# Mixture-of-experts start: an earlier place for the first expert's down weights, and its input gathered transposed in two halves

## What is computed

```python
h = h + hybrid_mixer(rms_norm(h, norm1_g[layer]), w_in[layer], ret_norm_g[layer], hgrn_norm_g[layer], w_out[layer], lb)
h = h + expert_choice_ffn(rms_norm(h, norm2_g[layer]), w_router[layer], w_gate[layer], w_up[layer], w_down[layer])

def expert_choice_ffn(xn, w_router, w_gate, w_up, w_down):
    affinity = jax.nn.softmax((xn @ w_router).astype(jnp.float32), axis=-1)
    gate, idx = lax.top_k(jnp.swapaxes(affinity, 1, 2), cap)          # 16 experts, 32 tokens each
    xe = jax.vmap(lambda xb, ib: xb[ib])(xn, idx)                     # the chosen rows
    hid = silu(einsum('becd,edf->becf', xe, w_gate)) * einsum('becd,edf->becf', xe, w_up)
    ye = einsum('becf,efd->becd', hid, w_down) * gate[..., None]
    return scatter_add(ye, idx)
```

## Time and profile before

| | us |
|---|---|
| median of 3 runs (1631.9 to 1633.9) | 1632.93 |
| profiled execution, its own time | 1631.66 |
| span of that execution in the trace | 1629.5 |
| PE busy | 1307.9 |
| PE weight loads busy | 924.8 |
| DVE busy | 575.2 |
| ACT busy | 455.2 |
| POOL busy | 137.7 |

### The profile page before, as it was taken

The page is one execution under the profiler, slowest core; times in us unless marked ns, Lnnn a source line. Parts: engine busy times, 40 slices in busy tenths (PEclk is TensorE's granted clock), DMA queues, the critical chain, the costliest instruction groups (busy, mean ns, idle before and its releaser), DMA issues.

```text
span 1629.5 us, 28377 instructions
## 1 busy us (share of the span) xinstructions
PE 1307.9 (80%) x12516; PEld 924.8 (57%) x12516; DVE 575.2 (35%) x879; ACT 455.2 (28%) x592; POOL 137.7 (8%) x169
## 2 busy tenths in 40 slices
PE   8999999999999987566566667999987566566565
PEld 7788889998989843223222233989853223222232
DVE  7984774765484520000000002584520001000001
ACT  6337653445555311001010012554311001010011
POOL 0220200000313000000000000304000000000000
PEclk9999999999999999989899788999999989898887
DMA  8334344545445899999999999335899999999997
GB/s 280 105 129 156 117 173 157 205 160 203 156 147 216 369 422 427 427 429 429 428 428 429 429 428 403 134 123 226 351 420 426 428 428 428 430 427 430 427 427 302
DMA packets 79504, 515.59 MB, mean 316 GB/s; under 512 B 6545, under 2 KB 6929, under 8 KB 54593
## 3 DMA queue, kind: packets, MB, share of 16 engines
q1 hardware_dynamic: 76000, 509.21, 76.7%
q0 software_dynamic: 912, 2.83, 0.5%
q10 hardware_dynamic: 2512, 2.36, 0.4%
HBM read 513.33 MB, written 1.05 MB: 316 GB/s over the span
## 4 chain that ended last, share of the span: by engine, by line
DMA 47%; PE 37%; DVE 10%; ACT 2%; issue 2%; SPq 1%; DVEq 0%; ACTq 0%
DMA board<-in_w_down 24%; DMA board<-in_w_gate 21%; PE dense L1769 7%; PE dense L1771 7%; PE dense L1770 7%; PE bank L2340 4%; PE bank L2370 2%; DVE ring_parts L1288 2%; ACT ring_parts L887 2%; DMA ring<-in_even_w_in 1%; DVE board L1572 1%; DVE board L1563 1%; PE dense L1792 1%; PE bank L2163 1%; PE bank L2310 1%
## 5 line engine op out<-in xcount | busy, mean ns | idle before, releaser
L2340 PE MATMUL bank<-ring,board 128*32 128x256 f32 x2688 | 209.6, 463 | 142.7 <-DMA ring<-in_w_up 87.0
L2340 PEld LDWEIGHTS bank<-ring,board 128*32 128x32 f32 x2688 | 91.0, 125 | 255.4 <-DMA ring<-in_w_up 108.1
L1111 ACT ACTIVATE board<-bank 128x256 f32<-128x256 f32 x32 | 12.3, 384 | 731.7 <-PE bank L2340 731.7
L1682 DVE TENSOR_TENSOR board<-board,bank 128x256 f32<-128x256 f32 x32 | 13.5, 421 | 554.3 <-ACT board L1111 554.3
L1288 DVE TENSOR_TENSOR ring_parts<-ring,ring_parts 128x4096 fp32r<-128x4096 f32 (+1 forms) x41 | 172.6, 4213 | 84.8 <-ACT ring_parts L887 84.7
L887 ACT ACTIVATE ring_parts<-ring 128x4096 fp32r<-128x4096 f32 (+1 forms) x47 | 161.5, 3438 | 117.0 <-DMA ring<-in_w_in 30.1
L1769 PE MATMUL dense<-board_parts,ring_parts 128*128 128x256 f32 x624 | 179.4, 287 | 0.6 <-DVE ring_parts L1288 0.6
L1771 PE MATMUL dense<-board_parts,ring_parts 128*128 128x256 f32 x624 | 176.6, 283 | 0.0
L2340 PE MATMUL bank<-board 128*32 128x256 f32 x1408 | 108.0, 459 | 69.6 <-DMA board<-in_w_up 40.9
L1769 PEld LDWEIGHTS dense<-board_parts,ring_parts 128*128 128x128 f32 x624 | 119.7, 192 | 2.1 <-issue 1.9
L2340 PEld LDWEIGHTS bank<-board 128*32 128x32 f32 x1408 | 51.1, 124 | 122.7 <-DMA board<-in_w_up 50.5
(11 more groups left out here) (354 smaller groups left out, 2067.7 us busy)
## 6 DMA issues: line engine op xcount, KB each, us to landing
ring<-in_w_gate SPq DMA_DIRECT2D x44, 2048.0 KB, 40.8
ring<-in_w_up SPq DMA_DIRECT2D x40, 2048.0 KB, 41.8
ring<-in_w_down SPq DMA_DIRECT2D x40, 2048.0 KB, 40.8
board<-in_w_up SPq DMA_DIRECT2D x24, 2048.0 KB, 40.7
board<-in_w_gate SPq DMA_DIRECT2D x20, 2048.0 KB, 41.2
board<-in_w_down SPq DMA_DIRECT2D x20, 2048.0 KB, 40.7
ring<-in_w_in SPq DMA_DIRECT2D x18, 2048.0 KB, 7.9
ring<-in_even_w_in SPq DMA_DIRECT2D x9, 2048.0 KB, 7.9
```

What stands on the lines that cost most here:

```text
L2340: last = mm(o.rearrange("p (m b) -> p m b", b=2), xeT[:, 4 * (j // 2) + k, :], cols.rearrange("p (m r b) -> p r m b", r=2, b=2)[:, q % 2], ...
```

## The change

Three things. (1) `rgT` moves from columns 4096 to 5120 of the work area to the first half of the columns of `xT` (from 17920), and `m_hi` becomes a list of four quarters, at 2048, 2560, 3072 and 15872; so neither lies in the place of unit 4 any more. (2) Unit 4's load waits for the last input projection alone. (3) The first expert's rows are gathered already turned: x is the weight operand (128 x 128, every eighth feature) and `cselr` the moving one (32 columns), eight products for each half of the features, straight into the layout of `xeT`; DVE multiplies each half by the gain. The second half is gathered between the first expert's units 0 and 1. The copy, the two transposes and the old gather of the first expert fall away.

```diff
-        rgT = area(4096, "p (h s) -> p h s", h=RH, s=S)
+        rgT = board[:, WORK:WORK + RH * S].rearrange("p (h s) -> p h s", h=RH)
-        m_hi = work_r[:, 2048:4096].rearrange("p (c s) -> p c s", c=8)
+        m_hi = [work_r[:, at:at + 512].rearrange("p (c s) -> p c s", c=2) for at in (2048, 2560, 3072, 15872)]
...
-                        if s == RING:
-                            sp.wait_ge(gm_sb, 4 * (l + 1))
-                        sp.wait_ge(*((unit_done, OUT2[l] + 1), (rp_ps, RH * (l + 1)), (ho_ps, l + 1), (lg_ps, l + 1))[s - RING])
+                        sp.wait_ge(*((unit_done, OUT2[l]), (rp_ps, RH * (l + 1)), (ho_ps, l + 1), (lg_ps, l + 1))[s - RING])
...
+                        high = m_hi[2 * k + b]
...
-                        own.link(v.tensor_copy(m_hi[:, both, :], mT[:, both, :]))
-                        tt(m_lo[:, both, :], mT[:, both, :], m_hi[:, both, :].bitcast(F32), ALU.subtract).then_inc(gm_sb, 1)
+                        own.link(v.tensor_copy(high, mT[:, both, :]))
+                        tt(m_lo[:, both, :], mT[:, both, :], high.bitcast(F32), ALU.subtract).then_inc(gm_sb, 1)
...
+                def first_input(half):
+
+                    dve.wait_ge(*((xe_ps, NE * l + 1) if half else (ge_ps, (NE + 1) * l + 2)))
+                    k = slice(4 * half, 4 * half + 4)
+                    tt(xeT[:, k, :], WB[1][:, 128 * half:128 * half + 128].rearrange("p (k c) -> p k c", k=4), g2[:, k, :],
+                       ALU.mult).then_inc((ge_sb, xe_sb)[half], 1)
...
-                chosen_rows(0)
-                expert_input(0)
+                first_input(0)
+                first_input(1)
                 choose(1)
...
+                def gather_turned(half):
+
+                    for k in range(4 * half, 4 * half + 4):
+                        for i in range(NT):
+                            last = mm(WB[1][:, CAP * k:CAP * k + CAP], x[:, i, :].rearrange("p (m k) -> p k m", k=DC)[:, k],
+                                      cselr[:, i, :], start=i == 0, stop=i == 1)
+                    last.then_inc((ge_ps, xe_ps)[half], 1)
...
-                    pe.wait_ge(xe_sb, one)
+                    pe.wait_ge(*((ge_sb, NE * l + 1) if first else (xe_sb, one)))
                     for j in range(4):
                         w = in_place(j)
+                        if first and j == 1:
+                            gather_turned(1)
+                        if first and j == 2:
+                            pe.wait_ge(xe_sb, one)
...
-                gather(0)
-                gathered(0)
+                pe.wait_ge(csel_sb, NE * l + 1)
+                gather_turned(0)
                 for e in range(HEAD_E):
-                    expert(e, 6 * e)
+                    expert(e, 6 * e, first=e == 0)
```

More of the change, by code:

```diff
@@ L2274, in _ @@
                     chunks = range(4 - 4 * n, 8 - 4 * n)
-                    rows_unit(OUT2[l] + n, [[t[:, c, :] for c in chunks] for t in (m_hi, m_lo)], n == 0, n == 1,
+                    rows_unit(OUT2[l] + n, [[m_hi[c // 2][:, c % 2, :] for c in chunks], [m_lo[:, c, :] for c in chunks]], n == 0, n == 1,
                               [[], [], [bank_read, at(mix_transposes, 0)], []] if n == 0 else [[], [], [], [first_rows]],
@@ L2320, in gathered, with expert @@
                     last.then_inc(xe_ps, 1)
-                def expert(e, j0, turn=None, more=True):
+                def gather_turned(half):
[4 more added lines that the diff above has]
+                    last.then_inc((ge_ps, xe_ps)[half], 1)
+                def expert(e, j0, turn=None, more=True, first=False):
                     one = e + (NE * l + 1)
```

## The result

The changed kernel takes 1639.38 us (median of 6 runs, 1637.7 to 1639.85) against 1632.6 of the kernel before: ratio 1.0038, interval [1.0028, 1.0048], so 0.38% slower; the medians lie 6.8 us apart. The forecast was 1632.2, with a range up to 1634.3.

The account below looks back on a forecast made before the run. The prediction took the expert stretches to be bound by the weight stream at about 428 GB/s. A gain of 0.36 us in each layer, 0.7 in all, off the 1632.93 median gave 1632.2 us, range 1630.0 to 1634.3.

Parts of the forecast that it names:

- The slower rival: Turned gather: weights 32 bytes apart double the loads; first products 1.6 us later, 5.0 us lost, 1637.9 us; chance 0.1.
- The prediction's own sign of being wrong: First expert's gather: a first half over 3.46 us and a dip behind unit 12 would show a slower outcome.
- the price of a half of the gather: Eight products on PE: 3.1 us for the first half, bounds 1.96 and 3.56; 1.96 for the second at full clock.
- one place of x per nanosecond: Old gather's strided reading: 128 pairs in 128 ns, against 122 ns per router load, so stride may cost nothing more.
- the clock: PE in the first expert's gather: granted clock 0.50 until 577.5 us, then 1.00.
- a cover that went: Second half of the gather: unit 12 issued 3.79 us after 11, hidden by the 4.9 us unit 11 feeds the stream.
- 0.36 us gained at 11: First expert's input: first products start 3.48 us after 574.31, 0.36 us earlier per layer; bounds 1.51 earlier, 0.10 later.
- The part that I priced at nothing: Unit 4's load, some 11 us earlier: closes the first dip, but gains nothing if the first products end as late.
- the two gates: Weight stream held by unit 4's load and by the end of the first expert's unit 0 on PE, which issues 11.

Follow-up runs that it names:

- run with eight times the columns: Changed kernel with the turned gather's moving operand repeated eight times, 256 columns instead of 32, same result; 1638.41 us, ratio 1.0026.
- turned gather alone: Kernel before with the first expert's rows gathered already turned, unit 4 waiting as it did; 1638.51 us, ratio 1.0039.
- only the stride taken away: Changed kernel with the turned gather's weights read from 128 neighbouring features instead of every eighth; 1634.66 us, ratio 1.0012.
- only the zeros added: Changed kernel with six more products of zeros on PE ahead of the gather; 1638.35 us, ratio 1.0033.
- early load alone: Kernel before with the new places, the merge and unit 4's earlier wait, but the old gather; 1631.15 us, ratio 0.9989.

## Why the prediction was wrong

**What held.** The experts' stretches are bound by the stream: what it lost in the two layers is what the time lost (8.6 and 8.2 us between the profiled executions). Unit 4's load goes out behind unit 0's, the dip there closes (431 GB/s), unit 7's issue is unchanged, and what the layer gets is decided by when unit 0 ends on PE and issues 11. The slower rival had the right place: strided weights in the first half, and 12 late behind the second. The prediction's own sign of being wrong came with it: a first half over 3.46 us.

**The step that failed: the price of a half of the gather.** I took 3.1 us at the low clock, with an upper bound of 3.56, and 1.96 us at full clock for the second half. Both took 4.01. The router's row was the nearest in shape, but its weights are contiguous. The rows for the stride were there, 128 against 60 ns in the earlier trace rows, and I argued them away: I reckoned one place of x per nanosecond from pairs and set it equal to the loads' own 122 ns. There are no pairs: the old gather runs through 128 places for one feature and then through 128 for the next, so it reads 256 single elements in 128 ns, 0.5 ns each. A strided weight load takes 4.01 us / 16 = 250 ns for 128, about 2 ns each, and what makes it four times as dear is not shown. Nor do the two rows compare like with like, as one stands at granted clock 0.50 and the other at 1.00. The trace of before had a clean row, the next expert's gather at 1.00:

```profile
585.44 2.03 PE L2310 MATMUL bank<-x,board 128*32 128x256 f32 x16
...
585.40:587.40 2.00, 2.00 (x21) 0.46 (x12) 0.42 (x1) 0.39 (x1) 0.00 (x0) 1.00 1.02 410
```

The strided operand costs 2.03 us there and 2.05 at 0.50, so it does not follow the clock, while the 60 ns of the experts' records become 114 at 0.50 (unit 0 of the changed kernel, 3.64 us / 32). That was the sign that the stride, and not the 32 columns of weights, set the old gather's price. The rule that I quoted against the change (the Trainium skill, "SBUF — State Buffer", section "Door 1: The DMA port swizzle (why `[64,N]` ≈ `[32,N]`)": full bandwidth needs two accesses or more to a 16-byte line) agrees with the runs to the step: 2.17 us at 8 bytes, 3.94 at 16, 4.01 at 32. I gave that rival 0.1.

**The second step that failed: the clock.** I let it rise at 577.5, as in the trace of before, and priced unit 0, the second half and unit 1 at full clock. In the changed kernel it stayed at 0.50 until 591.9: unit 0 took 3.64 us instead of 1.9. What PE does ahead of the rise is itself part of the change: 32 columns behind each load of 128 instead of 256 behind 32. The run with eight times the columns had the clock back at 579.4. But that this is the reason is not shown: the turned gather alone, with the same work on PE, was at 0.50 from 574.1 to 580.8 and at 1.00 from 581.0 to 584.3. Why the changed kernel's clock stayed low for 17 us in both layers is open.

**The two causes overlap.** Both halves of the changed kernel lay at 0.50, where neighbouring weights take 3.62 to 3.63 us, so there the stride itself added only 0.4 us to each. With the clock up it kept a half at 4.01 all the same, in the gather alone. With only the stride taken away the time came down to 1634.66 us, with a clock that rose sooner in that execution; with only the zeros added it stayed at 1638.35. How the loss divides between the two is not settled.

**And a cover that went.** I hid the second half behind the 4.9 us of unit 11, at 1.83 + 1.96 = 3.79 us. It became 4.01 + 3.64 - 0.1 = 7.5 us, 2.6 too many in each layer. The forecast's 0.36 us gained at 11 became about 2.3 lost.

The rival's price was off as well: it multiplied the strided loads by the low clock (5.1 us for the first half), and they take 4.0 at either clock; and it left units 0 and 1 at full clock. The two errors partly cancel in its 1637.9, so that its nearness to 1639.4 is in part luck.

**The part that I priced at nothing.** The early load alone measured 0.9989, where my sum had no gain without an earlier 11. The interval reaches from 0.3 to 3.3 us, and its profiled execution shows the dip moved and not gone, as the two gates would have it; where the gain of its faster runs arises is open. The range, too, is not what its working gives: 1631.4 to 1633.1 widened by 1 us is 1630.4 to 1634.1, and 1639.38 lies outside of either.

## What to carry to other kernels

Before a wait is opened, ask which gate the stream meets next: here the second gate was a PE step of 6 us, and the same change lengthened it. Price an operand by its access pattern and not by its shape alone: at the full clock, products with weights 16 or 32 bytes apart took twice as long as with neighbouring ones, a cost that a contiguous neighbour row cannot show. An operand whose price is the same at both clock levels is a sign of such a cost. And where the clock is at its lower level, price the steps behind a change at both levels: here unit 0 came out at 1.9 to 2.0 or at 3.2 to 3.6 us.

## What the runs showed of the hardware that I had not expected

- Products with strided weights do not follow the clock: 4.01 us for 16 records at 0.50 and at 0.99, while contiguous ones take 3.63 and 1.97.
- The granted clock can stay at 0.50 while the profile has PE busy for 16.45 of 16.9 us, with narrow products between the wide ones; in the run with wide moving operands it was at 1.00 after 579.4, and in the turned gather alone, with the same narrow products, from 581.0 to 584.3.
- The same kernel gets either clock from one layer to the next: unit 0 took 2.02 us in the first layer and 3.64 in the second of one execution.
